# Four-norm change to a two-layer hybrid backbone: root table loaded ahead, squares ordered before the next weight rounding, second block four parts behind the first

## What is computed

```python
def rms_norm(x, w):
    xf = x.astype(jnp.float32)
    y = xf * lax.rsqrt(jnp.mean(xf * xf, axis=-1, keepdims=True) + EPS)
    return (y * w.astype(jnp.float32)).astype(x.dtype)

for layer in range(DEPTH):                       # DEPTH = 2
    u  = rms_norm(h,  norm_mix_w[layer]) * (1.0 + sc1)  + sh1
    uc = rms_norm(hc, norm_mix_w[layer]) * (1.0 + csc1) + csh1
    y, yc = mixer(u, uc, ...)                    # layer 0: GLA + mLSTM, layer 1: neighbourhood attention
    h = h + g1 * y
    u = rms_norm(h, norm_ffn_w[layer]) * (1.0 + sc2) + sh2
    h = h + g2 * conv_ffn(u, ...)                # up (44 blocks), depthwise conv, gelu, gate, down (22 blocks)
    if need_ctx:                                 # layer 0 only: the same for the context tokens
        ...
return rms_norm(h, final_norm_w)
```

## Time and profile before

| | |
|---|---|
| median of 3 runs | 1854.38 us (1853.78 to 1856.28) |
| profiled execution | 1852.1 us, of which the span is 1850.3 us |
| PE busy | 1738.3 us (94% of the span) |
| PEld / DVE / ACT / POOL busy | 1435.2 / 850.0 / 740.0 / 541.4 us |
| HBM traffic | 182.6 MB, mean 99 GB/s |

### The profile page before, as it was taken

One profiled execution on the slowest core, in us unless ns is written; L12 is line 12 of the kernel. 1 busy time (PEld: TensorE's weight loads), 2 busy tenths in 40 slices (PEclk: granted clock), 3 DMA queues, 4 the chain that ended last, 5 costly groups with the idle time before them and its releaser, 6 DMA issues.

```text
span 1850.3 us, 26117 instructions
## 1 busy us (share of the span) xinstructions
PE 1738.3 (94%) x9598; PEld 1435.2 (78%) x9598; DVE 850.0 (46%) x1336; ACT 740.0 (40%) x1165; POOL 541.4 (29%) x251
## 2 busy tenths in 40 slices
PE   6899999998989999999999979999999799999997
PEld 1677888887768888888888867878567588888876
DVE  4678876666676544444324241000773522222343
ACT  2572434774232322233333343211883333334442
POOL 0123124462212323232322213222002244444442
PEclk9999999998989999999999978999999899999998
DMA  8323223443323343334221212212321132323221
GB/s 323 133 69 126 87 86 107 122 147 127 114 72 111 137 137 125 123 116 137 70 68 58 69 35 69 69 57 68 120 75 55 48 102 91 102 91 103 91 92 46
DMA packets 66584, 184.04 MB, mean 99 GB/s; under 512 B 5920, under 2 KB 26784, under 8 KB 65200
## 3 DMA queue, kind: packets, MB, share of 16 engines
q1 hardware_dynamic: 44784, 164.69, 26.2%
q10 hardware_dynamic: 21696, 17.88, 3.2%
HBM read 180.40 MB, written 2.15 MB: 99 GB/s over the span
## 4 chain that ended last, share of the span: by engine, by line
PE 78%; DVE 6%; ACT 3%; issue 1%; POOL 0%; ACTq 0%; DMA 0%; DVEq 0%; PEldq 0%; POOLq 0%
PE ps L1834 34%; PE ps L2224 13%; PE ps L1833 9%; PE ps L1847 4%; PE ps L1913 3%; PE ps L2221 3%; PE ps L2310 2%; PE ps L2323 2%; PE ps L2298 2%; PE ps L1803 1%; DVE later_norm_nt L1196 1%; PE ps L1919 1%; DVE u L1211 1%; PE ps L1926 1%; PE ps L1813 1%
## 5 line engine op out<-in xcount | busy, mean ns | idle before, releaser
L574 POOL TENSOR_TENSOR wsp<-raw,wsp 128x1024 fp32r<-128x1024 f32 x201 | 492.3, 2449 | 1246.5 <-ACT wsp L639 1246.2
L1834 PE MATMUL ps<-u,wsp 128*128 128x512 f32 x2712 | 808.1, 397 | 12.7 <-DVE u L1208 8.5
L1834 PEld LDWEIGHTS ps<-u,wsp 128*128 128x128 f32 x2712 | 513.9, 190 | 134.6 <-DVE u L1208 9.4
L639 ACT ACTIVATE wsp<-raw 128x1024 fp32r<-128x1024 f32 x201 | 213.4, 1062 | 532.7 <-PE ps L1834 432.3
L1833 PE MATMUL ps<-u,wsp 128*128 128x256 f32 x1464 | 410.0, 280 | 9.2 <-DVE u L1211 8.4
L2224 PE MATMUL ps<-hsp,wsp 128*128 128x512 f32 x1056 | 307.9, 394 | 2.2 <-DVE hsp L1638 2.2
L1833 PEld LDWEIGHTS ps<-u,wsp 128*128 128x128 f32 x1464 | 276.7, 189 | 12.5 <-DVE u L1211 6.9
L2224 PEld LDWEIGHTS ps<-hsp,wsp 128*128 128x128 f32 x1056 | 197.6, 188 | 50.5 <-issue 3.4
L1647 DVE SCALAR_TENSOR_TENSOR conv<-apad,vec,conv 128x770 f32<-128x770 f32 (+1 forms) x44 | 47.9, 1090 | 273.8 <-ACT conv L1011 273.7
L1638 DVE TENSOR_TENSOR hsp<-hid,hsp 128x768 fp32r<-128x768 f32 (+1 forms) x88 | 83.3, 947 | 192.1 <-ACT hsp L1033 190.7
L2221 PE MATMUL ps<-hsp,wsp 128*128 128x256 f32 x528 | 146.0, 280 | 1.4 <-DVE hsp L1638 1.3
(11 more groups left out here) (244 smaller groups left out, 1800.4 us busy)
## 6 DMA issues: line engine op xcount, KB each, us to landing
raw<-in_weights SPq DMA_DIRECT2D x281, 512.0 KB, 3.6
nab<-in_nabias ACTq DMA_DIRECT2D x32, 256.0 KB, 2.9
start_w<-in_start SPq DMA_DIRECT2D x6, 1024.0 KB, 20.7
h<-in_x SPq DMA_DIRECT2D x4, 768.0 KB, 13.0
mD<-rows_scratch ACTq DMA_DIRECT2D x12, 256.0 KB, 4.0
mqs<-rows_scratch ACTq DMA_DIRECT2D x12, 256.0 KB, 4.9
h<-in_x ACTq DMA_DIRECT2D x2, 1536.0 KB, 7.3
start_w<-in_start SPq DMA_DIRECT2D x4, 512.0 KB, 11.0
```

The source lines that it names most:

```text
L574: pool.tensor_tensor(wsp[:, s % 2, 1, :], raw[:, raw_index(s) % 4, :], wsp[:, s % 2, 0, :].bitcast(F32), ALU.subtract).then_inc(*own.one(l ...
L639: act.activation(wsp[:, s % 2, 0, :], raw[:, raw_s % 4, :], ACT.Copy).then_inc(*own.one(hi_ready))
L1834: mm = pe.matmul(lat, w, x[:, k, xp, toks], start=first, stop=last)
```

## The change

- `load_roots` takes a root of a constant into an unused tile, so that the table is loaded there. It stands at the kernel's start before the squares, at the start of both output projections, and in both feed-forwards after the last up block.
- In the output projections ACT's square of part `m - 1` stands ahead of the wait for block `m` and its rounding, and DVE's addition of square `m - 1` ahead of the wait for block `m` and the update.
- `two_blocks` takes the place of `first_part` and of the part-by-part waits in `features`: after norms 0 to 3, PE multiplies block 1 four parts behind block 0.
- In the first norm, `load_shift(1)` is issued ahead of scale 2 and x 2; ACT makes the high parts 0 and 1 before it waits for the scale sums; DVE takes the scales one part later (`k == 3`).

```diff
@@ sync
             load_x(0)
             load_x(1)
+            load_shift(1)
             load_scale(2)
             load_x(2)
             load_x(3)
-            load_shift(1)
@@ scalar
+            def load_roots():
+
+                act.wait_ge(ones_ready.sem, 2)
+                act.wait_ge(*own.last())
+                act.activation(table[:, :], epsc[:, :], ACT.Sqrt).then_inc(*own.one(act_own))
@@ scalar, out_projection
+                load_roots()
                 for m in range(N_OUT):
+                    if m:
+                        square(q, m - 1, toks, (f.out_updated.sem, m))
                     act.wait_ge(block_used.sem, s0 + m + 1)
                     high(s0 + m + 2)
-                    if m:
-                        square(q, m - 1, toks, (f.out_updated.sem, m))
                 square(q, KT - 1, toks, (f.out_updated.sem, KT))
@@ scalar, first norm
+            load_roots()
             for k in range(KT):
                 square(norm[0], k, all_tokens, (x_loaded[k // 2].sem, 16))
...
+            act.wait_ge(sh_ready.sem, 1)
+            high_parts(norm[0], shift(0, 0), all_tokens, range(2))
             act.wait_ge(sc_done.sem, 1)
-            act.wait_ge(sh_turned.sem, 1)
             act.activation(shrow[0:2, 0:512], ps[0:2, 7, :], ACT.Copy).then_inc(*own.one(scrow_ready))
             high(1)
-            act.wait_ge(sh_ready.sem, 1)
-            high_parts(norm[0], shift(0, 0), all_tokens)
+            high_parts(norm[0], shift(0, 0), all_tokens, range(2, KT))
@@ vector, first_operand
-                    if k == 2:
+                    if k == 3:
                         dve.wait_ge(sc_turned.sem, 1)
@@ vector, add_out
+                    if m >= 2:
+                        add_squares(norm[2 * layer + 1], m - 1, toks)
                     dve.wait_ge(block_used.sem, s0 + m + 1)
...
-                    if m >= 2:
-                        add_squares(norm[2 * layer + 1], m - 1, toks)
@@ tensor
+            def two_blocks(s, outs, q):
+
+                pe.wait_ge(lo_ready.sem, s + 1)
+                for kk in range(KT + 4):
+                    for b, k in ((0, kk), (1, kk - 4)):
+                        if not 0 <= k < KT:
+                            continue
+                        if b == 0:
+                            pe.wait_ge(*q.lo_ready.at(k + 1))
+                        elif k == 0:
+                            pe.wait_ge(lo_ready.sem, s + 2)
+                        lat, cx = outs[b]
+                        for a, (wp, xp) in enumerate(PASSES):
+                            w, first, last = wsp[:, (s + b) % 2, wp, tile(k)], k == 0 and a == 0, k == KT - 1 and a == 2
+                            if cx is not None:
+                                pe.matmul(cx, w, u[:, k, xp, CTX], start=first, stop=last, skip_group_check=True)
+                            mm = pe.matmul(lat, w, u[:, k, xp, LAT], start=first, stop=last, skip_group_check=True)
+                        if k == KT - 1:
+                            mm.then_inc(*own.one(block_used))
@@ tensor, feed_forward and q/k
-                for b in range(N_UP):
+                two_blocks(s_up, [(ps[:, b, :], cx_bank(b) if layer == 0 else None) for b in range(2)], n)
+                for b in range(2, N_UP):
                     up(b, 0)
...
+            two_blocks(S_QK, [(ps[:, n, :], None) for n in range(2)], norm[2])
+            for n in range(2, N_QK):
```

More of the change, by code:

```diff
@@ L213, in build @@
         sc_one = take("sc_one", [P, KT])
+        table = take("table", [P, 1])
         mdec = take("mdec", [P, 2, HEADS])
@@ L1942, in decay_inputs @@
                 mm.then_inc(*own.one(apre_done))
-            def first_part(n, k):
-                if k == 0:
-                    pe.wait_ge(lo_ready.sem, n + 1)
-                if n == 0:
-                    pe.wait_ge(*norm[0].lo_ready.at(k + 1))
-                for a, (wp, xp) in enumerate(PASSES):
-                    first, last, w = k == 0 and a == 0, k == KT - 1 and a == 2, wsp[:, n, wp, tile(k)]
-                    pe.matmul(cx_bank(n), w, u[:, k, xp, CTX], start=first, stop=last, skip_group_check=True)
-                    mm = pe.matmul(ps[:, n, :], w, u[:, k, xp, LAT], start=first, stop=last, skip_group_check=True)
-                if k == KT - 1:
-                    mm.then_inc(*own.one(block_used))
-            for k in range(KT + 4):
-                if k < KT:
-                    first_part(0, k)
-                if k >= 4:
-                    first_part(1, k - 4)
+            two_blocks(0, [(ps[:, n, :], cx_bank(n)) for n in range(2)], norm[0])
             pe.wait_ge(const_loaded.sem, 16 * 5)
@@ L2267, in _ @@
             normalise(norm[2], slice(0, N_TOK))
-            for n in range(N_QK):
-                if n >= 2:
-                    pe.wait_ge(qk_taken.sem, n - 1)
-                features(S_QK + n, 0, ps[:, n % 2, :], cx_bank(n) if n >= KT else None, u,
-                         norm[2].lo_ready if n == 0 else None)
+            two_blocks(S_QK, [(ps[:, n, :], None) for n in range(2)], norm[2])
+            for n in range(2, N_QK):
+                pe.wait_ge(qk_taken.sem, n - 1)
+                features(S_QK + n, 0, ps[:, n % 2, :], cx_bank(n) if n >= KT else None, u)
             for cg in range(2):
```

13 lines of the change are left out of this document (5 added, 8 removed).

## The result

| | kernel before | changed kernel |
|---|---|---|
| median of four runs each | 1855.33 us (1853.78 to 1857.42) | 1841.10 us (1838.99 to 1843.97) |
| profiled execution: time, span | 1852.1, 1850.3 us | 1841.93, 1840.1 us |
| TensorE's granted clock over the span | 0.965 | 0.968 |

The ratio is 0.9924 (95% 0.9906 to 0.9942): faster by 14 us, where 32 were predicted, and outside the range of 1816 to 1834. Which chip this first comparison ran on is not on record.

The account below looks back on a forecast made before the run. PE, holding 78% of the chain, was taken to bound the kernel, with time to gain only in its waits at the norms. 8.4 + (6.1 + 4.0) + (1.3 + 3.1) + (6.2 + 1.4) + 1.3 = 31.8 us gave 1822.6 us, range 1816 to 1834.

Parts of the forecast that it names:

- passes through: Layer 0's up and down products: PE is always busy, so whatever is gained before them reaches the end.
- the prediction's own signs of being wrong: Sums at the low clock, output-projection steps holding PE between blocks, or the first norm's gain gone at 200 us.
- The first norm, 8.4: First norm: 2.9 from earlier shift rows, 5.2 from earlier high parts, 0.3 from PE's start; 8.4 us (5 to 9.5).
- The ACT order: First norm: high part 0 directly follows the shifts, so DVE goes on some 5 us sooner; 5.2 us.
- The earlier shift rows: First norm: shift transfers land at 18.8, so PE's sums start at 25.8 instead of 29.02; 2.9 us taken.
- Norm 1's squares, 6.1: Norm 1: squares beside the last block let DVE start parts near 508.0, not 514.13; 6.1 us (4.2 to 7.4).
- norm 3's, 6.2 with its table load: Norm 3: parts start from 1449.7 instead of 1455.88, the table load included; 6.2 us (5.0 to 7.2).
- The blocks, 4.0 + 3.1 + 1.4: Second block four parts behind the first: 4.0 us after norm 1, 3.1 after norm 2, 1.4 after norm 3.
- The table, 1.3 each: Norms 2 and 4: no 1.28 us table load between sums and root any more; 1.3 us gained in each.
- What the earlier steps cost, nothing: Output projections: earlier squares and additions delay no block; cost nothing, at most 2 us with no slack left.
- The clock takes part of it back: Rival, chance 0.16: an earlier clock fall doubles sums, spreads and tails of blocks 0 and 1; near 1832 us.
- Late weights and a table load in the wrong place: Two rivals, together 0.16: blocks 2 and 3 wait for POOL, 1827 us; a load still before the root, 1826.5.

Follow-up runs that it names:

- before_b: The kernel before, unedited, run and profiled once more: 1858.55 us.
- after_c: The changed kernel, unedited, run again beside the kernel before: 1839.96 us over six runs, ratio 0.9888.
- squares_only: The kernel before with only ACT's square and DVE's addition moved ahead of the wait in both output projections: 1851.24 us, ratio 0.9952.
- table_last: The changed kernel with the new table tile put at the end of memory: 1841.90 us, ratio 0.9892.
- first_only: The kernel before with only the first norm's three edits (early shifts, early high parts 0 and 1, later scales): 1855.36 us, ratio 0.9961.
- fill_four: The changed kernel with four unread PE products between the first norm's shift rows and sums: 1832.67 us over six runs, ratio 0.9851.
- blocks_only: The kernel before with only blocks 0 and 1 four parts apart after norms 1, 2 and 3: 1860.74 us, ratio 1.0003.
- fillers: The changed kernel with late shift loads restored and unread PE products in norms 0 to 3: 1833.83 us, ratio 0.9853; repeated, 1838.13 us, 0.9884.
- no_first: The changed kernel without the first norm's three edits: 1846.70 us, ratio 0.9910.

## Why the prediction was wrong

**The base of the sum.** The forecast for the profiled execution was 1820.3 us and the execution took 1841.9. Of the 21.6 us between them 14.0 lie in the free stretches and 7.6 in the norms. The step that failed most is therefore the one that makes the sum against the single profiled execution, as if the lengths of its free stretches were properties of the kernel: they were put at no change, and the runs showed a spread of 8 us before mark 31 and two lengths, 6.5 us apart, from 41 to 104. The profile of before had drawn the quick pace and the shortest stretch of all before mark 31; against `before_b` its free stretches were 9.6 us short in all. The other 4.4 are the changed kernel's own draw, whose 381.59 before mark 31 is the longest of the 16.

That a gain "passes through" was not what failed: 22 of the 24 us in the norms show in the medians of the later sets. I took 8.32 us a block for the price of a block. Its 1.04 us a part stood within 2% of the other draw and did no harm in the sum; as the base of a forecast to 0.2% it cost 10 us. The three runs of before then known (1853.78 to 1856.28) gave no warning. Why all four of them in that set lie in the lowest quarter of the 58 measured later (1850.17 to 1871.47, median 1861.0) is open. Chance alone would do that to four independent runs once in some 250 sets, so something that this set shared, a chip for instance, is not excluded; no run here tests it.

Two of the prediction's own signs of being wrong were seen. The sums ran at the low clock in the first norm (next paragraph). And in the first pair the gain of the first norm is gone at 200 us: mark 15, at 202.82 before, comes 0.8 us later in the changed kernel. But in `after_c` it comes 3.0 us sooner than before, and `before_b` is 2.9 us behind the first profile of before by mark 17, without any change. So this second sign was set off by a stretch that varies by itself.

**The first norm, 8.4.** The trace shows 3.6 at the first low part and 2.5 at mark 2. The ACT order gave 5.1 of the 5.2 predicted. The earlier shift rows gave nothing where 2.9 us stood, and this term is the second step that failed. I had written the bound "no gain, if the clock has fallen by the sums" and taken the other end. My own sum should have warned me: shift rows that land at 18.8 and take 3.6 us are done near 22.4, and the squares end at 25.7, an idle gap of more than 3 us, in a kernel whose clock fell 4.7 us after real work. The first low part came at 47.36 where "near 43" was written. Of the last 1.1 us (3.6 at the first low part, 2.5 at mark 2) DVE lost 0.35, since its last low part starts 3.25 us sooner (63.56 against 66.81): `amod`, 0.17 us before and 1.53 now, took over from low part 0 the place beside POOL's split. The rest, 0.75, lies on PE, which had parts of both blocks in hand and the low clock, where before it had idle time and the full one. Its window just ahead of the last parts, now and then before:

```profile
60.00:62.00 2.00, 2.00 (x6) 0.50 0.01 4
```

```profile
60.00:62.00 2.00, 1.26 (x6) 1.00 0.00 0
```

**Norm 1's squares, 6.1; norm 3's, 6.2 with its table load.** 5.5 and 6.2 in the traces (7.9 behind the last block instead of 13.4; 5.7 instead of 11.8). In norm 1 the second twelve sums began at the full clock and ended at the low one, 2.13 instead of 1.36. Right, and confirmed by `squares_only`.

**The blocks, 4.0 + 3.1 + 1.4.** Block 1 ended about 26.8 us after DVE's start, by the working above, where I had 26.5. The working of the new order was right; the old one was over-priced, since the low clock in the tail of block 0 was that execution's. Against it the change gained 3.3 us in norm 1 between DVE's start and mark 41, against the three other executions of that code 2.3; in norm 2 2.5 to 3.5, in norm 3 0.8. The third block's wait for POOL, 0.4 us, came as worked out.

**The table, 1.3 each.** The spread of norm 4 waited 1.90 us before and waits 0.62 after, a difference of 1.28. The Trainium skill (ScalarE: Activation LUTs, What ACT_TABLE_LOAD costs) adds a drain of some 1380 ns to each load; the trace shows none of it here, and what the load took is what its removal gave.

**What the earlier steps cost, nothing.** Right: blocks of the output projection end without a gap, with DVE's reduction at 3.44 us. They end every 8.48 us in the profile after and every 8.32 in `after_c`, the two paces again.

**The rivals.** "The clock takes part of it back" came true in the first norm, 3 to 4 us of it, and for 0.8 us in the second twelve sums of norm 1. Late weights and a table load in the wrong place did not occur. That the change slows the stages behind it was the reading that the first pair of profiles suggested, and it fell with `before_b`.

By its own terms: 24 us in the norms instead of 31.8 (first norm 5.9 short, norm 1 1.2, norm 3 0.6), and 22 in the medians of the later sets. From 1861 that is 1837 to 1839, near where the changed kernel stands. The first comparison's 14 us differ from these 22 mostly by its quick executions of before (1855.3 against 1861), and little by the changed kernel (1841.1 against 1839 to 1840). With the usual base the forecast of 31.8 us would still have promised 8 to 10 us more than there was.

## What to carry to other kernels

Before a forecast of a per cent is made from one profile, take a second profile of the same kernel and compare stages that nobody touches: their spread is the error of the base. Work that is moved forward on an engine gains only if what comes behind it is ready too. Here an idle gap of 3.7 us on TensorE ahead of twenty-four small matmuls brought them the low clock (up to 5.4 instead of 3.0 us), and four dummy products in that gap put the kernel 2 to 3 us ahead in the traces; its median stood 7 us lower, in one set. Where a wait cannot be avoided, fill it at the place that sets the end, not where another engine sets the pace.

## What the runs showed of the hardware

**Two steady paces at the full clock.** A pair of 256 and 512 columns started every 0.347 or every 0.353 us, with granted clock 1.00 and PE 100% busy, fixed for hundreds of microseconds and different from one execution of a kernel to the next, or between two stages of one execution (`before_b`). The Trainium skill (TensorE: Matmul & The Clock Gate, Back-to-back issue gap) gives N / 2.4 + 2.5 ns for an isolated matmul at the full clock; an estimate by that rule is 325 ns for the pair. It says as well that in a stream of weight loads and matmuls the spacing is another, 131 ns at N = 512. Both measured paces lie above the rule, a latent block here took 5.44 / 24 = 0.227 us for each matmul of 512 columns, far above that 131 ns, and neither figure has a second pace. What selects the pace was not found; it is not the memory layout (`before` and `before_b`, `table_last`, `first_only`).

**Sums do not hold the clock.** Matmuls with two columns kept PE busy by the profile, and the clock fell during or right behind them in the first norm (near 29 in `fill_four`) and in norm 1 with every gap filled. It does not always: in the first norm of before, `before_b`, `blocks_only`, `fillers` and `no_first` the rows behind the same twenty-four sums took 3.6 us, at the full clock.

**A tiny DVE operation beside POOL.** 8 columns took 0.17 us alone and 1.53 us beside a POOL subtraction. It ended when POOL's did: 52.22 + 1.53 = 53.75 against 51.34 + 2.38 = 53.72. So here its length was what was left of POOL's operation, not a share of its own.
